# A conformer and GLA trunk on one core: conv taps without GpSimd, input and output by channel

## The reference

```
u = h @ w_pw1 + b_pw1
a, gate = split(u, 2)
u = a * sigmoid(gate)
full = concatenate([state, u], axis=1)
c = depthwise_conv(full, w_dw) + b_dw          # 31 taps a channel
c = silu(layer_norm(c, ln_g, ln_b))
y = c @ w_pw2 + b_pw2
```

## Time and profile before

| | us |
|---|---|
| median of three runs | 2202.49 (2202.31 to 2202.76) |
| the profiled execution | 2202.91 |
| its span, first to last instruction | 2201.2 |
| TensorE busy | 2120.0 |
| VectorE busy | 1038.1 |
| ScalarE busy | 721.6 |
| GpSimd busy | 259.0 |
| mean granted clock of TensorE | 0.984 |

### The profile page before, as it was taken

How to read it: one execution, slowest core, us unless ns; L and a number is a source line. 1 busy time by engine, 2 the same in 40 slices (tenths; PEclk the granted TensorE clock), 3 DMA queues, 4 the chain that set the end, 5 groups by cost and what they waited for, 6 DMA issues and landing times.

```text
span 2201.2 us, 39380 instructions
## 1 busy us (share of the span) xinstructions
PE 2120.0 (96%) x16192; PEld 2070.6 (94%) x16192; DVE 1038.1 (47%) x1298; ACT 721.6 (33%) x1095; POOL 259.0 (12%) x214
## 2 busy tenths in 40 slices
PE   8999999988789999999999999999999899999997
PEld 8999999978679999999999999999987799999997
DVE  4555533389956444433344443333456364444332
ACT  5222222476643222222322222222333242222222
POOL 0000001277604000001100000220000040000000
PEclk9999999999889999999999999999999999999999
DMA  5233222211113222233232223323224133222321
GB/s 158 87 88 92 83 82 86 89 48 49 39 41 109 86 86 86 84 88 88 82 97 86 86 86 89 87 84 87 67 59 134 58 108 94 86 86 86 96 80 67
DMA packets 339452, 185.65 MB, mean 84 GB/s; under 512 B 6874, under 2 KB 335804, under 8 KB 339356
## 3 DMA queue, kind: packets, MB, share of 16 engines
q1 hardware_dynamic: 336268, 173.03, 27.1%
q0 software_dynamic: 2848, 11.39, 1.5%
q10 hardware_dynamic: 256, 0.10, 0.0%
HBM read 177.29 MB, written 8.05 MB: 84 GB/s over the span
## 4 chain that ended last, share of the span: by engine, by line
PE 87%; DVE 5%; issue 2%; POOL 2%; ACT 2%; DMA 0%; SPq 0%; ACTq 0%; DVEq 0%; POOLq 0%
PE ps L435 78%; PE ps L456 4%; POOL pool_sum L837 2%; DVE w_lo L422 1%; DVE ps L1447 1%; ACT w_hi L415 1%; PE ps L1123 1%; PE ps L964 1%; PE ps L1129 0%; PE ps L952 0%; PE ps L1036 0%; PE ps L1062 0%; DMA pin<-in_gla_onorm_g 0%; PE ps L1070 0%; DVE uext L1486 0%
## 5 line engine op out<-in xcount | busy, mean ns | idle before, releaser
L435 PE MATMUL ps<-xg_hi,w_hi 128*128 128x272 f32 x3344 | 698.1, 290 | 4.1 <-DVE ta L1582 2.2
L435 PE MATMUL ps<-xg_hi,w_lo 128*128 128x272 f32 x3344 | 693.6, 289 | 0.0
L435 PE MATMUL ps<-xg_lo,w_hi 128*128 128x272 f32 x3344 | 691.4, 288 | 0.0
L415 ACT ACTIVATE w_hi<-raw 128x1024 fp32r<-128x1024 f32 x329 | 347.5, 1059 | 999.7 <-PE ps L435 950.9
L422 DVE TENSOR_TENSOR w_lo<-raw,w_hi 128x1024 fp32r<-128x1024 f32 x329 | 427.5, 1301 | 451.4 <-ACT w_hi L415 450.9
L435 PEld LDWEIGHTS ps<-xg_hi,w_hi 128*128 128x128 f32 x3344 | 529.3, 189 | 8.0 <-issue 4.6
L435 PEld LDWEIGHTS ps<-xg_lo,w_hi 128*128 128x128 f32 x3344 | 527.5, 189 | 0.0
L435 PEld LDWEIGHTS ps<-xg_hi,w_lo 128*128 128x128 f32 x3344 | 523.9, 190 | 0.0
L435 PE MATMUL ps<-h_hi,w_hi 128*128 128x272 f32 x1536 | 318.2, 288 | 1.7 <-DVE x L1526 0.9
L435 PE MATMUL ps<-h_hi,w_lo 128*128 128x272 f32 x1536 | 318.0, 288 | 0.0
L435 PE MATMUL ps<-h_lo,w_hi 128*128 128x272 f32 x1536 | 316.7, 288 | 0.0
(11 more groups left out here) (258 smaller groups left out, 1447.5 us busy)
## 6 DMA issues: line engine op xcount, KB each, us to landing
raw<-in_ffn_w_gate SPq DMA_DIRECT2D x88, 512.0 KB, 3.8
raw<-in_ffn_w_up SPq DMA_DIRECT2D x88, 512.0 KB, 3.8
raw<-in_ffn_w_down SPq DMA_DIRECT2D x64, 512.0 KB, 3.7
raw<-in_gla_w_in SPq DMA_DIRECT2D x25, 512.0 KB, 3.8
...
raw<-in_conv_w_pw SPq DMA_DIRECT2D x24, 512.0 KB, 3.8
raw<-in_gla_w_out SPq DMA_DIRECT2D x8, 512.0 KB, 3.6
...
```

Of the source, the lines that this page charges most:

```text
L415: nc.scalar.activation(w_hi[:, n % RING], raw[:, n % RAW], ACT.Copy).then_inc(w_high, 1)
L435: last = nc.tensor.matmul(ps[:, 2 * pair + c, 0:HALF], w[:, r, k, :], a[:, k0 + k, c * HALF:(c + 1) * HALF], start=(k0 + k == 0 and w is w ...
```

## The change

**Input and constants.** The host lays x out by channel, eight blocks of 128 x 544, all gains and biases as one table of 128 x 110 and the taps as one of 128 x 248. ScalarE's queue loads the table, blocks 0 to 2 of x and the taps; SyncE loads blocks 3 to 7 behind the first two weight slots. All transposes and copies of the head are gone. Squares of blocks 0 to 5 are summed by GpSimd, those of 6 and 7 by ScalarE and VectorE, and the statistics stand behind slot 2 instead of in front of it; the first norm's factors are formed in full width like the later ones.

**Conv.** TensorE has 7 taps (8 and 15 in the last two blocks), each as one product in full fp32, 128 x 512, from uext itself; u_hi, u_lo and the split taps are gone. ScalarE has one tap, with the bias, and VectorE the other 23 (22 and 15). GpSimd has none. For the samples ScalarE writes four products a block into a table samp, beside the history's part, and VectorE reduces it over its five columns.

**Output.** The last down product keeps its four pairs of banks and has no transposes. Block 7 is computed half by half of the columns (66 products each); in each half the square of block 7 is added to GpSimd's sum by a product with ones, the factors are formed in a width of 272, VectorE writes five blocks of y and GpSimd three that ScalarE scaled by the gain before. y goes out by channel, four stores a half, and the host transposes it.

The core of the diff (of most hunks the new lines only; the old ones stand above):

```diff
-    PE_TAPS = [6] * (M - 2) + [7, 14]
-    POOL_TAPS = [12] * (M - 2) + [12, 8]
-    DVE_TAPS = [TAPS - a - b for a, b in zip(PE_TAPS, POOL_TAPS)]
+    PE_TAPS = [7] * (M - 2) + [8, 15]
+    DVE_TAPS = [TAPS - a - 1 for a in PE_TAPS]
     tap_base = [sum(DVE_TAPS[:m]) for m in range(M + 1)]
-    pool_base = [sum(POOL_TAPS[:m]) for m in range(M + 1)]
-    PRODS = 6
     POOL_SQ = (1, 3, 5)
     PE_SQ = tuple(m for m in range(M) if m not in POOL_SQ)
-    DIAG_HALF = 8
-    DIAG_LAST = M * BLK // (P * 4) // 2 - DIAG_HALF
-    diag = at("diag", [P, DIAG_HALF + DIAG_LAST, 2, P], F32R, HHI)
-    tap_prod = at("tap_prod", [P, PRODS, SEQ], F32, HLO)
+    DIAGS = M * BLK // (P * 4) // 2
+    assert max(PE_TAPS) <= DIAGS
+    diag = at("diag", [P, 2, DIAGS, P], F32, HHI)
...
+    HEAD_X = 3
+    HEAD_SQ = 6
...
+                if m == 0:
+                    for b in range(HEAD_X, M):
+                        sp.dma_start(x[:, b, :], x_by_channel[b]).then_inc(s_x[b], 16)
...
-            pe.wait_ge(evac, 2)
-            pe.wait_ge(s_xo, 2)
             wide_products(pe, s0, [u0 % 4, (u0 + 1) % 4], xg_hi, xg_lo, (x_split, 0))
-            pe.wait_ge(s_diag, TT + 1)
-            bank = 2 * ((u0 + 3) % 4)
-            for t in range(TT):
-                nc.tensor.matmul(ps[:, bank, t * P:(t + 1) * P], ones[:, :], rdiag[:, t, :], start=True, stop=True)
-            nc.tensor.matmul(ps[:, bank + 1, 0:NS], ones[:, :], rdiag[:, TT, 0:NS], start=True, stop=True).then_inc(
-                s_stat, 1)
             slot_products(pe, s0 + 2, (u0 + 2) % 4, xg_hi, xg_lo)
-            pe.wait_ge(s_r0, 1)
+            pe.wait_ge(s_acc, 1)
+            pe.wait_ge(s_sum, 1)
+            for c in range(2):
+                cols = slice(c * HALF, (c + 1) * HALF)
+                for term in (acc, sqt):
+                    last = nc.tensor.matmul(ps[:, 2 * ((u0 + 3) % 4) + c, 0:HALF], ones[:, :], term[:, cols],
+                                            start=(term is acc), stop=(term is sqt))
+            last.then_inc(s_stat, 1)
+            pe.wait_ge(s_nv, 1)
...
+            for m in range(M):
+                for c in range(3):
+                    high(act, s0 + 3 * m + c + AHEAD)
+                if m in POOL_Y:
+                    act.wait_ge(evac, u0 + m + 1)
+                    nc.scalar.activation(y[:, m, :], x[:, m, :], ACT.Copy,
+                                         scale=par[:, C_FIN + m:C_FIN + m + 1]).then_inc(f_pre, 1)
+            for c in range(2):
+                cols = slice(c * HALF, (c + 1) * HALF)
+                act.wait_ge(f_x, c + 1)
+                nc.scalar.activation(ta[:, 0, cols], x[:, M - 1, cols], ACT.Square).then_inc(f_sq, 1)
+                act.wait_ge(f_nv, 3 * c + 1)
+                nc.scalar.activation(ns[:, cols], nv[:, cols], ACT.Ln).then_inc(f_seed, 1)
+                act.wait_ge(f_seed, 2 * c + 1)
+                nc.scalar.activation(rB[:, cols], ns[:, cols], ACT.Exp, scale=-0.5).then_inc(f_seed, 1)
+                act.wait_ge(f_yp, c + 1)
+                act.dma_start(y_by_channel[POOL_Y[0]:POOL_Y[-1] + 1, :, cols].rearrange("m p t -> p m t"),
+                              y[:, POOL_Y[0]:POOL_Y[-1] + 1, cols]).then_inc(f_outa, 16)
...
+                if m < M - 1:
+                    dve.wait_ge(w_done, s0 + 3 * m + 3)
+                    nc.vector.scalar_tensor_tensor(
+                        out=halves(x[:, m, :]), in0=bank_pair((u0 + m) % 4), scalar=0.5,
+                        in1=halves(x[:, m, :]), op0=ALU.mult, op1=ALU.add).then_inc(evac, 1)
+            for c in range(2):
+                cols = slice(c * HALF, (c + 1) * HALF)
+                dve.wait_ge(f_half, c + 1)
                 nc.vector.scalar_tensor_tensor(
+                    out=x[:, M - 1, cols], in0=ps[:, 2 * ((u0 + M - 1) % 4) + c, 0:HALF], scalar=0.5,
+                    in1=x[:, M - 1, cols], op0=ALU.mult, op1=ALU.add).then_inc(f_x, 1)
+                dve.wait_ge(f_stat, c + 1)
+                nc.vector.tensor_scalar(nv[:, cols], ps[:, 2 * FINAL_PAIR + c, 0:HALF], EPS, None,
+                                        ALU.add).then_inc(f_nv, 1)
+                dve.wait_ge(f_seed, 2 * c + 2)
+                nc.vector.scalar_tensor_tensor(out=ns[:, cols], in0=rB[:, cols], scalar=-0.5, in1=rB[:, cols],
+                                               op0=ALU.mult, op1=ALU.mult).then_inc(f_nv, 1)
+                dve.wait_ge(f_nv, 3 * c + 2)
+                nc.vector.tensor_tensor(ns[:, cols], ns[:, cols], nv[:, cols], ALU.mult).then_inc(f_nv, 1)
+                dve.wait_ge(f_nv, 3 * c + 3)
+                nc.vector.scalar_tensor_tensor(out=rB[:, cols], in0=ns[:, cols], scalar=1.5, in1=rB[:, cols],
+                                               op0=ALU.add, op1=ALU.mult).then_inc(f_rb, 1)
+                dve.wait_ge(f_rb, c + 1)
+                for m in DVE_Y:
+                    nc.vector.scalar_tensor_tensor(
+                        out=y[:, m, cols], in0=x[:, m, cols], scalar=par[:, C_FIN + m:C_FIN + m + 1],
+                        in1=rB[:, cols], op0=ALU.mult, op1=ALU.mult).then_inc(f_y, 1)
...
+        for c in range(2):
+            cols = slice(c * HALF, (c + 1) * HALF)
+            for i, (a, b) in enumerate(((0, 2), (2, 4), (M - 1, M))):
+                sp.wait_ge(f_y, len(DVE_Y) * c + (2, 4, 5)[i])
+                sp.dma_start(y_by_channel[a:b, :, cols].rearrange("m p t -> p m t"), y[:, a:b, cols]).then_inc(
+                    f_out, 16)
...
-        load_taps(pool, 1, s_inp)
-        load_vectors(pool, PAR_ROWS[4:8], s_inp)
         nc.gpsimd.memset(hist_prod[:, :, :, :], 0.0).then_inc(c_zero, 1)
-        pool.wait_ge(u_init, M)
+        pool_square_sum(pool, x, 0, lambda m: (s_x[m], 16), HEAD_SQ)
...
+        nc.gpsimd.memset(samp[:, :, :, :], 0.0).then_inc(c_zero, 1)
...
+        pool_square_sum(pool, x, 6, lambda m: (evac, f11.down.u0 + m + 1), M - 1)
+        pool.wait_ge(f_pre, len(POOL_Y))
+        for c in range(2):
+            cols = slice(c * HALF, (c + 1) * HALF)
+            pool.wait_ge(f_rb, c + 1)
+            for m in POOL_Y:
+                last = nc.gpsimd.tensor_tensor(y[:, m, cols], y[:, m, cols], rB[:, cols], ALU.mult)
+            last.then_inc(f_yp, 1)
...
             pe.wait_ge(c_diag, m + 1)
             wait(pe, c_fin, m - 1)
-            n, half = PE_TAPS[m], diag_first(m)
-            for js in (range(half), range(half, n)):
-                if js and js[0]:
-                    pe.wait_ge(c_diag, m + 2)
-                for part in range(2):
-                    for j in js:
-                        last = nc.tensor.matmul(ps[:, 4 + m % 2, :], diag[:, diag_slot(m, j), part, :],
-                                                u_hi[:, m % 2, j:j + SEQ], start=(j == 0 and part == 0), stop=False)
-                if js and not js[0]:
-                    pe.wait_ge(c_ulo, m + 1)
-                for j in js:
-                    last = nc.tensor.matmul(ps[:, 4 + m % 2, :], diag[:, diag_slot(m, j), 0, :],
-                                            u_lo[:, m % 2, j:j + SEQ], start=False, stop=(j == n - 1))
+            n = PE_TAPS[m]
+            for j in range(n):
+                last = nc.tensor.matmul(ps[:, 4 + m % 2, :], diag[:, m % 2, j, :], uext[:, m, j:j + SEQ],
+                                        start=(j == 0), stop=(j == n - 1))
             last.then_inc(c_pe, 1)
...
+        for slot in range(3):
+            last = half_products(0, slot)
+        last.then_inc(f_half, 1)
+        half_products(1, 0)
+        pe.wait_ge(evac, u0 + M - 3)
+        pe.wait_ge(s_acc, 7)
+        final_stat(0, acc)
+        final_stat(1, acc)
+        pe.wait_ge(f_sq, 1)
+        final_stat(0, ta[:, 0, :]).then_inc(f_stat, 1)
+        for slot in range(1, 3):
+            last = half_products(1, slot)
+        last.then_inc(f_half, 1)
+        pe.wait_ge(f_sq, 2)
+        final_stat(1, ta[:, 0, :]).then_inc(f_stat, 1)
...
+        act.dma_start(par[:, :], vectors).then_inc(s_par, 16)
+        for b in range(HEAD_X):
+            act.dma_start(x[:, b, :], x_by_channel[b]).then_inc(s_x[b], 16)
+        act.dma_start(wdw[:, :], taps_by_channel).then_inc(s_taps, 16)
         act.preload_act_table_set(LN_EXP)
         high(act, 0)
+        act.wait_ge(s_par, 16)
+        for m in range(M):
+            act.wait_ge(s_x[m], 16)
             nc.scalar.activation(xg_hi[:, m, :], x[:, m, :], ACT.Copy, scale=par[:, m:m + 1]).then_inc(x_high, 1)
+            if m == 0:
+                high(act, 1)
         high(act, 2)
+        for m in range(HEAD_SQ, M):
+            nc.scalar.activation((ta if m == HEAD_SQ else tb)[:, 0, :], x[:, m, :], ACT.Square).then_inc(s_sq, 1)
...
+            last = nc.scalar.activation(diag[:, m % 2, j, :], ident[:, :], ACT.Copy, scale=tap(j, m))
+            if j == PE_TAPS[m] - 1:
+                last.then_inc(c_diag, 1)
...
             act.wait_ge(c_u, m + 1)
             wait(act, c_fin, m - 3)
+            i = PE_TAPS[m]
```

(79 more changed lines are left out.)

360 lines of the change are left out of this document (71 added, 289 removed).

## The result

**Measured:** 2207.1 us median (2205.0 to 2208.5, 20 runs) against 2202.1 (2199.9 to 2203.6, 20 runs) for the kernel before. The ratio is 1.0021, 95% interval 1.0015 to 1.0027: slower by 0.21%. That is 5.0 us, just over the 4.4 us that the prediction called the least that a measurement can tell from no change. The forecast was 2208.2. The profiled execution took 2207.2 us, its span 2205.5, 4.3 more than before.

The account below looks back on a forecast made before the run. TensorE, busy 96% of the span, sets most of the time; the change touches only head, conv stage and tail. -3.7 + 12.7 - 3.3 = +5.7 us: 2208.6 profiled, 2208.2 median, range 2198.5 to 2215.5.

Parts of the forecast that it names:

- Conv stage, +12.7: Conv stage: VectorE still sets the pace, blocks of 23.2 us instead of 21.7; +12.7 us, bounds +10 to +17.
- The two terms without a row of their own: Conv stage: a full-precision product of 512 columns put at 0.86 us, a reduction of 160 elements at 0.25 us.
- the order of time: Conv stage: count following instructions from first uext (433.3) to last addition (619.4 against 606.68), giving +12.7 us.
- work and waits: Conv stage, VectorE: +17.1 us work, less 15 of old waits, plus 9 new before the second uext: +11.
- Head, -3.7: Start of the kernel: first product at 11.4 us, slot 3 ending at 42.5 against 46.1; -3.7 us, bounds -8.1 to 0.
- the catch, the turns: Head: VectorE's w_lo and xg_lo and GpSimd's square sum block each other, 1.06 us more for a VectorE instruction.
- Tail, -3.3: End of the kernel: last product 1.9 us earlier, then 12.8 us behind it instead of 14.25; -3.3 us, bounds -5.6 to -0.5.
- No turns: Rival, head and tail: VectorE and GpSimd do not block each other; -1.0 us, 2201.5; chance 0.25.
- The bound of -8.1: Head, low bound: without VectorE and GpSimd blocking each other, first product at 8.8 us; -8.1 us.
- TensorE as the bound by its clock: Rival, conv stage: TensorE at its lower clock sets the pace; two blocks lost, +28 us, 2236; chance 0.07.
- New waits in a block: Rival, conv stage: VectorE waits for c_pe or ScalarE's samples, 0.6 to 1 us a block; 2212.5 to 2214.5; chance 0.18.

Follow-up runs that it names:

- Experiment 5: Changed kernel with 9 taps a block on TensorE (10 and 16 in the last two) instead of 7 (8 and 15), taken from VectorE: 2197.2 us, ratio 0.9974.
- experiment 7: Changed kernel with ten taps a block on ScalarE, nine additions on GpSimd, 14 taps on VectorE, still seven on TensorE: 2171.5 us, ratio 0.9856.
- experiment 3: Changed kernel with GpSimd's first square sum held until VectorE has written all eight xg_lo: 2207.8 us, ratio 1.0024 to the kernel before.
- experiment 4: Changed kernel with all eight y of each half on VectorE and none on GpSimd: 2206.4 us, ratio 1.0017 to the kernel before.
- experiment 6: Changed kernel with 11 taps a block on TensorE (12 and 16 in the last two), taken from VectorE: 2202.3 us, ratio 1.0000 to the kernel before.

## Why the prediction was right

For the profiled execution +5.7 was forecast and +4.3 measured. Nearly all of the 1.4 between them is the head's.

**Conv stage, +12.7; measured +12.6.** The sum was right in its steps, not only in its total. The forecast's times in this stage were told on the clock of the kernel before, with the head apart; so, with the head's 4.84 us added, the trace has the first uext at 433.30 (forecast 433.3), the second at 451.3 (451.4), the last at 590.4 (590.6), the final addition at 619.3 (619.4). Period 23.19 against 23.2. The two terms without a row of their own held: a full-precision tap took 6.01 / 7 = 0.859 us (0.86 from the columns of the sum over partitions), and the reduction took 0.31 by itself but 0.23 from start to start (0.25, taken between the small steps and the wide one). Counting the order of time instead of the sum of work was the right choice: work and waits had given +11. Experiment 5 shows the mechanism: two tap steps fewer shortened the period by two steps, 1.58 us. One premise was loose. The prediction asks whether VectorE still sets the pace, but before the change the pace came from VectorE together with GpSimd and ScalarE (experiment 7). This did no harm, because the count took the old period from the trace.

**Head, -3.7; measured -4.84.** The direction and the chain were right, three terms were off. Slot 0's weights landed at 5.2, not 6.2, and its w_lo and xg_lo took 1.85 and 1.63 instead of 2.3 and 1.85, so the first product started at 9.8 instead of 11.4. The split of slot 1 was done at 12.0, not 13.7, and from there TensorE needed 14.33 us for the 90 products that were left, where 15.0 had been counted; so the wide slots ended at 26.4 instead of 28.7. As forecast, it started slowly: 12 products took 2.7 us up to 17.9 and 1.5 after that, which is close to the two levels of the clock, though the granted clock in the profile reads 1.00 throughout. Against this the statistics took 1.85 and not 0.95: the row of 0.92 us is for two products, and the new code has four, which was a miscount. The two errors have opposite signs (-2.3 and +0.9), and that much of the head's closeness is luck. What the prediction called the catch, the turns, was real but nearly free here: experiment 3 takes them away, ends the wide slots 0.7 us earlier, and loses that again to the late sum.

**Tail, -3.3; measured -3.45.** The last product came 2.0 earlier (forecast 1.9), and 12.8 us lie behind it (12.8). Inside, the terms offset each other: VectorE took up the last half 1.2 us late rather than 1.7 (2193.94 against 2192.7), the steps to the first y took 4.5 (4.25), the y 3.75 (4.3), and from the last y at 2202.2 to the end were 3.3 us (2.5).

**The rivals.** *No turns* (2201.5) is refuted by its own signs, as the first product started at 9.8 and the wide slots ended at 26.4, not before 9 and 25, and by the timelines of experiments 3 and 4: the turns are there. Its price was too high even so. The bound of -8.1 let all 96 products follow the first one at 8.8, but 90 of them wait for slot 1 (11.54 in experiment 3). *TensorE as the bound by its clock* (2236) did not come: granted clock 0.92 over the stage, and it rose to 0.99 and 1.00 when experiments 5 and 6 filled the idle time. TensorE can be made the bound, by work: at eleven taps. *New waits in a block* (2212.5 to 2214.5) did not come either: VectorE's rows show none in a block (2.8 us in all in front of taps, in block 1, where the prediction had TensorE set the pace).
